# Short runs of columns in the matmuls' access patterns of a two-layer decoder step

## The reference

```python
def short_conv_mixer(h, prev, w_in, w_dw, w_out):      # w_in 1024 x 3072, w_out 1024 x 1024
    b_gate, c_gate, v = jnp.split(h @ w_in, 3, axis=-1)
    u = c_gate * v
    uc, st = causal_dwconv(u, prev, w_dw)
    return (b_gate * uc) @ w_out, st

def sb_mixer(...):                                     # w_qkv 1024 x 3072, w_o 1024 x 1024
    qkv = h @ w_qkv                                    # then attention
    return o @ w_o, k, v

def conv_ffn(h, prev, w_up, w_dw, b_dw, w_down):       # w_up 1024 x 5632, w_down 2816 x 1024
    g, u = jnp.split(h @ w_up, 2, axis=-1)
    gc, st = causal_dwconv(g, prev, w_dw)
    return (jax.nn.silu(gc + b_dw) * u) @ w_down, st

# per layer: x = x + mixer(rmsnorm(x)); x = x + conv_ffn(rmsnorm(x)); a last rmsnorm at the end
```

## Time and profile before

| | |
|---|---|
| time, median of 2 runs | 2621.59 us (2619.81 to 2623.36) |
| span of the profiled execution, first to last instruction | 2615.1 us |
| what the median has beyond that span | 6.5 us |
| PE busy | 2570.0 us, 98% of the span, 16982 matmuls |
| DVE, ACT, POOL busy | 53%, 21%, 27% |
| matmuls of `three` (L543, L546, L547, with 352 columns) | 14112 |

### The profile page before, as it was taken

One profiled execution on the slowest core, in us unless ns is written; L12 is line 12 of the kernel. 1 busy time (PEld: TensorE's weight loads), 2 busy tenths in 40 slices (PEclk: granted clock), 3 DMA queues, 4 the chain that ended last, 5 costly groups with the idle time before them and its releaser, 6 DMA issues.

```text
span 2615.1 us, 40858 instructions
## 1 busy us (share of the span) xinstructions
PE 2570.0 (98%) x16982; PEld 2443.8 (93%) x16982; DVE 1374.5 (53%) x1346; ACT 550.8 (21%) x1145; POOL 708.4 (27%) x405
## 2 busy tenths in 40 slices
PE   8999999999999999999999999999999999999997
PEld 7999999999999999988888888669999999999996
DVE  5333446444544444476667666654644455444445
ACT  4000221000000000144444444542100000000012
POOL 3333333323322333322111111013332332233331
PEclk9999999999999999999999999999999999999999
DMA  4111111111111111122111111641111111111111
GB/s 142 43 47 49 47 44 49 41 49 48 42 41 49 49 49 49 44 70 95 35 40 36 39 42 42 211 172 41 49 41 49 49 41 41 49 49 49 49 44 67
DMA packets 62523, 149.06 MB, mean 57 GB/s; under 512 B 5666, under 2 KB 28962, under 8 KB 62370
## 3 DMA queue, kind: packets, MB, share of 16 engines
q1 hardware_dynamic: 56130, 130.35, 15.6%
q10 hardware_dynamic: 6240, 16.36, 1.6%
HBM read 128.91 MB, written 17.78 MB: 56 GB/s over the span
## 4 chain that ended last, share of the span: by engine, by line
PE 92%; DVE 5%; issue 2%; ACT 1%; POOL 1%; DMA 0%; DVEq 0%; POOLq 0%; ACTq 0%; SPq 0%
PE bank L543 28%; PE bank L547 28%; PE bank L546 27%; PE bank L807 2%; PE bank L745 2%; DVE prod L1591 2%; PE bank L778 2%; DVE beta L1595 1%; PE bank L680 0%; PE bank L748 0%; DVE h_lo L1432 0%; DVE rstd L1366 0%; PE bank L881 0%; PE bank L912 0%; POOL w_lo L521 0%
## 5 line engine op out<-in xcount | busy, mean ns | idle before, releaser
L543 PE MATMUL bank<-h_hi,w_hi 128*128 128x352 f32 x3648 | 1189.0, 326 | 14.4 <-DVE h_lo L1352 7.6
L547 PE MATMUL bank<-h_hi,w_lo 128*128 128x352 f32 x3648 | 1175.2, 322 | 0.0
L546 PE MATMUL bank<-h_lo,w_hi 128*128 128x352 f32 x3648 | 1171.6, 321 | 0.0
L506 POOL CAST w_hi<-raw 128x1024 fp32r<-128x1024 f32 x194 | 212.5, 1095 | 1841.9 <-PE bank L543 1795.2
L543 PEld LDWEIGHTS bank<-h_hi,w_hi 128*128 128x128 f32 x3648 | 685.0, 188 | 24.2 <-issue 14.8
L546 PEld LDWEIGHTS bank<-h_lo,w_hi 128*128 128x128 f32 x3648 | 689.0, 189 | 0.8
L547 PEld LDWEIGHTS bank<-h_hi,w_lo 128*128 128x128 f32 x3648 | 685.1, 188 | 0.0
L508 POOL TENSOR_TENSOR w_lo<-raw,w_hi 128x1024 fp32r<-128x1024 f32 x194 | 478.4, 2466 | 15.5
L1486 DVE TENSOR_TENSOR x<-x,bank 128x1056 f32<-128x1056 f32 x174 | 218.3, 1254 | 320.5 <-PE bank L547 318.6
L543 PE MATMUL bank<-a_hi,w_hi 128*128 128x352 f32 x1056 | 343.7, 325 | 2.3 <-POOL w_lo L508 2.3
L546 PE MATMUL bank<-a_lo,w_hi 128*128 128x352 f32 x1056 | 340.8, 323 | 0.0
(11 more groups left out here) (129 smaller groups left out, 1622.3 us busy)
## 6 DMA issues: line engine op xcount, KB each, us to landing
raw<-weights SPq DMA_DIRECT2D x196, 512.0 KB, 3.5
x_spill<-x ACTq DMA_DIRECT2D x8, 528.0 KB, 5.1
k_out<-k_t ACTq DMA_DIRECT2D x8, 528.0 KB, 3.1
v_out<-v_t ACTq DMA_DIRECT2D x8, 528.0 KB, 2.7
x<-x_spill SPq DMA_DIRECT2D x8, 528.0 KB, 7.3
pages_hi<-cache_k SPq DMA_DIRECT2D x8, 512.0 KB, 6.0
pages_hi<-cache_v SPq DMA_DIRECT2D x8, 512.0 KB, 7.2
pages_lo<-cache_k SPq DMA_DIRECT2D x8, 512.0 KB, 7.4
```

What stands on the lines that cost most here:

```text
L506: nc.gpsimd.tensor_copy(w_hi[ring][:, :], raw[slot][:, :]).then_inc(w_high, 1)
L543: mm = nc.tensor.matmul(o, w_hi[w][:, c0:c0 + P], hi, start=first, stop=False)
L546: nc.tensor.matmul(o, w_hi[w][:, c0:c0 + P], lo, start=False, stop=False)
L547: return nc.tensor.matmul(o, w_lo[w][:, c0:c0 + P], hi, start=False, stop=last)
```

## The change

`linear` and `down` hand `three` a pair (places, run). The 352 columns of the output and of both moving operands are then seen as `places` equal pieces, and the matmul goes over them in short runs: `run` columns of the first piece, `run` of the second, and so on over all pieces, then the next `run` of each. Output and moving operands are walked alike, so each column's result lands where it did. The stationary operand stays as it is. With (2, 2) the columns come as 0, 1, 176, 177, 2, 3, 178, 179, ...; with (11, 2) as 0, 1, 32, 33, 64, 65, ... through eleven places 32 columns apart.

| stage | function | places, run | pieces are apart by |
|---|---|---|---|
| sc_in | `linear` | 2, 2 | 176 columns |
| sc_out | `linear` | 2, 4 | 176 |
| ffn0 up | `linear` | 2, 16 | 176 |
| ffn0 down | `down` | 11, 4 | 32 |
| wo | `linear` | 4, 2 | 88 |
| ffn1 up | `linear` | 11, 2 | 32 |
| ffn1 down | `down` | 2, 8 | 176 |

`first_linear`, `last_linear`, `last_down`, `project` and all other matmuls are as before. No instruction is added, removed or moved on any engine.

```diff
+WALK = {"sc_in": (2, 2), "sc_out": (2, 4), "wo": (4, 2), "ffn0": (2, 16), "ffn1": (11, 2)}
+DOWN_WALK = {"ffn0": (11, 4), "ffn1": (2, 8)}
...
-            def three(o, w, c0, hi, lo, first, last, counts=False):
-
+            def walked(ap, walk):
+                apart, run = walk
+                return ap.rearrange("p (a b c) -> p b a c", a=apart, c=run)
+
+            def three(o, w, c0, hi, lo, first, last, counts=False, walk=None):
+
+                if walk is not None:
+                    o, hi, lo = (walked(t, walk) for t in (o, hi, lo))
                 mm = nc.tensor.matmul(o, w_hi[w][:, c0:c0 + P], hi, start=first, stop=False)
...
-            def linear(tile, ring, s, fill, midway=None):
+            def linear(tile, ring, s, fill, walk, midway=None):
...
-                                   h_lo[:, k, tokens(j)], k == 0, k == KC - 1, k == j == 0)
+                                   h_lo[:, k, tokens(j)], k == 0, k == KC - 1, k == j == 0, walk)
...
-                        linear(tile0 + k, (tile0 + k) % SPLIT, s, fill)
+                        linear(tile0 + k, (tile0 + k) % SPLIT, s, fill, WALK[name])
...
-                        linear(tile + n, (ring0 + n) % SPLIT, s, fill,
+                        linear(tile + n, (ring0 + n) % SPLIT, s, fill, WALK[name],
...
-                                   j == 0 and (f, kk) in (order[0], release))
+                                   j == 0 and (f, kk) in (order[0], release), DOWN_WALK[name])
...
-                        linear(tile, n % SPLIT, s, fill, {1: first_sums, 2: first_means}.get(tile))
+                        linear(tile, n % SPLIT, s, fill, WALK["sc_in"], {1: first_sums, 2: first_means}.get(tile))
```

## The result

The changed kernel takes **3340.8 us** (median of 2 runs, 3340.58 to 3341.01) against 2621.59: a ratio of 1.275, 95% interval 1.271 to 1.279. The forecast was 2622 us with a range of 2610 to 2900. It was wrong: 719 us slower, and outside the range.

What follows compares the result with a forecast made beforehand. The prediction took PE's pace through the matmuls of `three` to bound the kernel. Its sum was 2621.6 + 11520 x 0 = 2622 us, with a range of 2610 to 2900.

Steps and rivals of the forecast that it cites:

- What bounds the kernel: Whole span: PE is busy 98%, so the matmuls of `three` times their 160 ns pace set the time.
- I take zero for a jump: In the 11520 walked matmuls, jumping between short runs was taken to cost PE nothing, adding 0 us.
- the 0.044 ns from which it decides: Cost per short run in walked matmuls that would make a 2% change, 52.4 us; a tenth of a column's 0.45.
- Neighbours by pairs stay together in both memories, in all seven patterns: Walked operands and outputs: even-length runs on even columns keep pairs together, favouring zero cost for a jump.
- the quotation that stands behind it: Trainium skill on PSUM cachelines of 8 bytes: every two consecutive elements should be contiguous; read as making all walks free.
- The first rival: Walked matmuls: each jump costs, reading or writing; half a column adds 269 us, a whole one 538; chance 0.20.
- The second rival: sc_in, wo, ffn1 up: runs of 2 use half of each SBUF read, 295 ns a matmul, 690 us; chance 0.07.
- The third rival: All 11520 walked matmuls: any pattern with jumps goes at half rate, 1555 us more, 4177 us; chance 0.04.
- Faster: Walked matmuls lose some of the 12.5 ns outside their columns; all of it is 144 us, 2478; chance 0.05.
- Range: Whole kernel, 8 in 10: 2610, from the spread of stretches, to 2900, past half a column per run (2891).

## Why the prediction was wrong, point by point

- **What bounds the kernel**: right. PE's pace alone sets the time, no other engine took part, and the counts held: 11520 matmuls, 11.5 us for each nanosecond.
- **"I take zero for a jump"**: this is the step that failed. The evidence was DVE's small copies, which bounded a jump to 1.8 ns on another engine; measured on PE, a run of two columns costs 0.38 to 0.95 ns (67 to 167 ns over 176), inside that bound and 9 to 22 times the 0.044 ns from which it decides. In the change's runs of 4 to 16 it is 0.08 to 0.25 ns (7 ns over 88 to 5.6 over 22), some 44 us in all, and the zero was nearly right. What is paid for in the runs of 2 isn't the turn but the group of 16 bytes that is used by half: the order 0 2 1 3 turns more often and is at 158.9 ns.
- **"Neighbours by pairs stay together in both memories, in all seven patterns"**: true, and enough for the writes only (ratio 1.0007). For reads it wasn't enough: pairs alone in their group of 16 bytes are at 226 to 327 ns in the change, aligned fours at 167 to 168. The sentence took one unit for both memories; the quotation that stands behind it is about PSUM alone.
- **The first rival** (a cost for each run, in the ratio of runs): wrong in kind. It made sc_out, with 88 runs, half as dear as sc_in; measured were 8 ns and 67, and wo and ffn1 up, with as many runs as sc_in, over twice its price.
- **The second rival** (half-used reads, only runs of 2): this was the mechanism, with its place and nearly its sum, 690 us for 719. Its chance of 0.07 was far too low: all seven runs and blocks were aligned, so the one thing that set three stages apart from the rest was half a group of 16 bytes, and the rival named it. What it had as its price, 295 ns for all three, was 225.6, 305.7 and 326.9: too high where the walk comes back to a group after one pair, too low elsewhere. Over its 5112 matmuls the mean is 294 ns by the table; that this meets the 295, which was read from float32 records, is luck as far as these runs show. Also it had the longer runs free; they add 44 us by the table.
- **The third rival** (half rate for any pattern with jumps): fell. The 6408 matmuls in runs of 4 to 16 are at 166 to 168 ns.
- **Faster**: nothing of it. No pattern went below the paces of the kernel before (158.9 ns).
- **Range**: it ended at 2900 because the first rival's middle did. The step from the chances to the range was sound; the chances weren't. A case that moves 5112 matmuls to half rate was put at 0.07 on a guess about which of two memories is tolerant, when no row speaks of either.

## What to carry to other kernels

An output walked in aligned runs of 2 to 16 columns costs these matmuls nothing that was measurable (runs of one column weren't tried), so where columns must be reordered, reorder them in the write, in pairs, and read the moving operand straight. If the read must be permuted, keep each aligned 16 bytes together, four float32 columns (the order 0 2 1 3 was as good as 0 1 2 3); below that a float32r matmul of 160 ns took 226 to 372, and nothing hides it in a kernel that stands on PE. And when a cost that no row shows multiplies with 11520 instructions on the path, one stage's worth of that instruction tried alone is worth more than any argument from another engine.

## What the runs showed of the hardware beyond that

- A group of 16 bytes left for one pair of columns and taken up again costs about half of what a fresh one does: 226 to 229 ns at four distances, against 306 to 333. One left for two pairs is saved as well: two places in shifted runs of 4 are at 230. Left for three pairs, it is lost (306 with four places).
- Sixteen places are at 368 to 372 ns, less than half rate; other patterns of half groups lie between 306 and 333 without an order that these runs explain.
- The clock fell in one slow pattern, for a cause that stays open. In the run with sixteen places 24 apart, the stretches before were at full clock, at 307 ns with PE busy without a gap; in each of ten stretches with the sixteen places the granted clock fell to the 1.2 GHz level and the pace was 427 ns, and it came back after each. Window length, PE busy, clock, DMA:

```profile
640.00:690.00 50.00, 50.00 (x165) 1.00 0.06 21
690.00:751.00 61.00, 61.00 (x144) 0.53 0.03 9
752.00:839.00 87.00, 87.00 (x285) 0.99 0.10 31
```

PE counts as busy for all of the 61 us, so the busy share doesn't tell of it; the granted clock has to be read beside it. With sixteen places 20 and 22 apart, at 368 and 372 ns, the clock stayed at full speed, so a slow read alone doesn't bring it about.
